# A chunked delta rule on one NeuronCore: the triangular inverse of levels 0 to 4 kept as 32-column blocks, and one set of square sums issued a chunk earlier

## The reference

```python
    sol = lax.linalg.triangular_solve(m, rhs, left_side=True, lower=True, unit_diagonal=True)
    u, w = sol[..., :dv], sol[..., dv:]
    qk = jnp.einsum('bhnid,bhnjd->bhnij', q, k) * decay
```

## Time and profile before

| | us |
|---|---|
| median of 3 runs | 1479.24 |
| the profiled execution, its own time | 1478.25 |
| its span, first to last instruction | 1476.4 |
| projection stage | up to about 344 |
| delta stage, four tiles | about 344 to 554 |
| its tail, mixing, experts, combining | the rest |
| mean granted TensorE clock | 0.988 |

### The profile page before, as it was taken

The page is one execution under the profiler, slowest core; times in us unless marked ns, Lnnn a source line. Parts: engine busy times, 40 slices in busy tenths (PEclk is TensorE's granted clock), DMA queues, the critical chain, the costliest instruction groups (busy, mean ns, idle before and its releaser), DMA issues. The chain is left out here.

```text
span 1476.4 us, 21155 instructions
## 1 busy us (share of the span) xinstructions
PE 1437.6 (97%) x8144; PEld 1143.3 (77%) x8144; DVE 973.3 (66%) x1765; ACT 625.8 (42%) x963; POOL 356.8 (24%) x236
## 2 busy tenths in 40 slices
PE   8999999998999999999899999999999999999986
PEld 6999999987998898788767667667667667767732
DVE  6648877515667676046978767767767767767628
ACT  3565333414244423011125555555555565565400
POOL 0000000004234340002463333333333333334200
PEclk9999999979999999999999999999999999999999
DMA  6222222210000002800739999999999999999767
GB/s 226 72 72 86 86 85 85 86 32 16 1 2 2 30 1 83 328 29 5 285 122 382 365 374 375 372 369 368 375 375 363 366 364 366 374 367 364 264 254 319
DMA packets 55932, 313.32 MB, mean 212 GB/s; under 512 B 15200, under 2 KB 16224, under 8 KB 36640
## 3 DMA queue, kind: packets, MB, share of 16 engines
q1 hardware_dynamic: 36080, 276.19, 49.5%
q0 software_dynamic: 19760, 35.89, 6.5%
HBM read 301.37 MB, written 42.12 MB: 233 GB/s over the span
## 5 line engine op out<-in xcount | busy, mean ns | idle before, releaser
L393 PE MATMUL bank<-x_hi,w_hi 128*128 128x274 f32 x768 | 230.4, 300 | 0.0
L2294 POOL DMA_INDIRECT expert_rows<-lru,slot_ids x64 | 155.9, 2435 | 297.8 <-DVE lru L2515 286.2
L395 PE MATMUL bank<-x_hi,w_lo 128*128 128x274 f32 x768 | 225.4, 294 | 0.0
L394 PE MATMUL bank<-x_lo,w_hi 128*128 128x274 f32 x768 | 224.5, 292 | 0.0
L2508 DVE TENSOR_TENSOR gate_up_lo<-wide,gate_up_hi 128x2048 fp32r<-128x2048 f32 x84 | 192.1, 2287 | 40.4 <-ACT gate_up_hi L2448 40.4
L2373 PE MATMUL bank<-gate_up_hi,rows_hi 128*128 128x512 f32 x512 | 206.3, 403 | 0.0
L2374 PE MATMUL bank<-gate_up_lo,rows_hi 128*128 128x512 f32 x512 | 200.3, 391 | 0.0
L2375 PE MATMUL bank<-gate_up_hi,rows_lo 128*128 128x512 f32 x512 | 200.0, 391 | 0.0
L2448 ACT ACTIVATE gate_up_hi<-wide 128x2048 fp32r<-128x2048 f32 x84 | 161.1, 1919 | 0.0
L394 PEld LDWEIGHTS bank<-x_lo,w_hi 128*128 128x128 f32 x768 | 147.7, 192 | 0.3
L393 PEld LDWEIGHTS bank<-x_hi,w_hi 128*128 128x128 f32 x768 | 146.9, 191 | 1.1 <-DVE w_lo L603 0.5
(11 more groups left out here) (358 smaller groups left out, 2583.0 us busy)
## 6 DMA issues: line engine op xcount, KB each, us to landing
wide<-in_w_exp SPq DMA_DIRECT2D x43, 2048.0 KB, 15.0
kept_wide<-in_w_exp SPq DMA_DIRECT2D x21, 2048.0 KB, 14.8
w_out_first<-in_w_in SPq DMA_DIRECT2D x48, 512.0 KB, 3.5
wide<-in_w_exp SPq DMA_DIRECT2D x22, 1024.0 KB, 13.1
w_out_first<-in_w_exp SPq DMA_DIRECT2D x21, 1024.0 KB, 13.4
kept_rows<-in_w_exp SPq DMA_DIRECT2D x21, 1024.0 KB, 13.3
expert_rows<-expert_rows SPq DMA_DIRECT2D x5, 1536.0 KB, 21.5
wide<-in_w_out SPq DMA_DIRECT2D x5, 1024.0 KB, 10.0
```

The source lines that it names most:

```text
L393: nc.tensor.matmul(out, wh[:, k, :], x_hi[:, k, at], start=(k == 0), stop=False)
L394: nc.tensor.matmul(out, wh[:, k, :], x_lo[:, k, at], start=False, stop=False)
L395: last = nc.tensor.matmul(out, wl[:, k, :], x_hi[:, k, at], start=False, stop=(k == DC - 1))
L2294: return pool.indirect_dma_start(out=dram["expert_rows"], out_offset=bass.IndirectOffsetOnAxis(ap=index, axis=0), in_=source, in_offset=No ...
```

## The change

In the projection stage the sums of tile 0 move from chunk 43 to chunk 42, and VectorE's read of them from its turn 44 to its turn 43.

In the delta stage, levels 0 to 4 no longer keep 128 by 128 inverses. After level 4 the inverse is block diagonal with blocks of 32, so each head's inverse is kept as 128 rows by 32 columns (`x_p`, and `x_t_p` for the transposed one). GpSimd masks `lower_t` to its 32 by 32 blocks (`mask_blocks`, in place of `begin_inverse`). TensorE then multiplies the 128 by 128 weights with 32 moving columns; VectorE's first half reads the product with a broadcast that spreads the 32 columns over four blocks; its second half subtracts 32 columns, and a 32 by 32 block transpose on VectorE (`turn_blocks`) gives `x_p`. TensorE's turn and ScalarE's copy are left at level 5 alone. Before level 5, GpSimd spreads both forms to 128 columns (`spread_inverse`, eight operations of 128x256). The transpose of level 0's second half becomes a matmul with a 32-column identity. The sample's first inverse (L1380) moves from VectorE to GpSimd. Smaller: one bias tile is four times narrower and read with a broadcast, the rows of log decays of the next tile wait for the last block product, and the constants grow by 160 columns.

```diff
-                project(pe, 40 + j, j, between={3: sum_prompt, 5: sum_sample}.get(j))
+                project(pe, 40 + j, j, between={2: sum_prompt, 5: sum_sample}.get(j))
...
-                elif n == 44:
+                elif n == 43:
                     rf.read(dve, 0)
...
+        lower_few_rows = carve(few_work, 0, H, BLOCK)
+        block_lower, rg_few = rg, o_sq
+        x_p = carve(mem.kept_wide, 4 * H * P, H, BLOCK)
+        x_t_p = [carve(work, 5 * H * P, H, BLOCK), *[lower_few_rows] * (TILES - 1)]
...
             def join_product(t, level):
...
+                        if level > SMALL:
+                            last = nc.tensor.matmul(inverse_bank(t, q, w)[:, h, :], lower_t[0:w, n, 0:w], x_inv[0:w, n, 0:w],
+                                                    start=True, stop=True)
+                        elif level:
+                            last = nc.tensor.matmul(blocks_out(t, q, 0)[:, h, :], block_lower[:, n, :], x_p[:, n, :],
+                                                    start=True, stop=True)
...
             def join_applied(t, level):
...
-                            last = nc.tensor.transpose(out, left, C("ident")[0:w, 0:w])
+                            last = nc.tensor.matmul(blocks_out(t, q, 1)[:, h, :], joined[:, n, :],
+                                                    x_t_p[t][:, n, :] if level else eye_p, start=True, stop=True)
...
-                    if 0 < level < LEVELS - 1:
-                        turn_inverse(t, level)
+                    if level == SMALL + 1:
+                        turn_inverse(t)
...
+            def mask_blocks(t):
+
+                for g, hs in groups:
+                    pool.wait_ge(s_u, 2 * turn(t) + g + 1)
+                    pool.tensor_tensor(block_lower[:, hs, :], lower_t[:, hs, :],
+                                       mem.delta_consts("blocks").unsqueeze(1).to_broadcast([P, 4, P]), ALU.mult)\
+                        .then_inc(s_bl, 1)
+
+            def spread_inverse(t):
+
+                mask = mem.delta_consts("blocks").unsqueeze(1).to_broadcast([P, 2, P])
                 for q, hs in pairs:
+                    pool.wait_ge(s_x, inverse_steps(t, SMALL, q))
+                    for small, out in ((x_p, x_inv), (x_t_p[t], x_inv_t[t % 2])):
+                        pool.tensor_tensor(by_block(out[:, hs, :]), spread(small[:, hs, :]), by_block(mask), ALU.mult)\
+                            .then_inc(s_un, 1)
...
                     scale_masks(t, 2, 3)
                     square_o(t - 1)
                     scale_masks(t, 4, 5)
+                    spread_inverse(t)
                     scale_o(t - 1)
...
             def join(t, level):
...
+                    if 0 < level <= SMALL:
+                        nc.vector.tensor_tensor(by_block(joined[:, hs, :]), spread(blocks_out(t, q, 0)), by_block(mask[:, hs, :]),
+                                                ALU.mult).then_inc(s_p, 1)
...
+                    for q, hs in pairs:
+                        dve.wait_ge(s_px, inverse_steps(t, level, q))
+                        nc.vector.tensor_tensor(x_t_p[t][:, hs, :], x_t_p[t][:, hs, :] if level else eye, blocks_out(t, q, 1),
+                                                ALU.subtract).then_inc(s_xtp, 1)
+                        if q:
+                            turn_blocks(t, level, q - 1)
+                    turn_blocks(t, level, 3)
                 after_joining(t, level)
+
+            def turn_blocks(t, level, q):
+
+                at = slice(2 * BLOCK * q, 2 * BLOCK * q + 2 * BLOCK)
+                dve.wait_ge(s_xtp, 4 * (SMALL + 1) * t + 4 * level + q + 1)
+                nc.vector.transpose(x_p.rearrange("p h c -> p (h c)")[:, at],
+                                    x_t_p[t].rearrange("p h c -> p (h c)")[:, at]).then_inc(s_x, 1)
```

More of the change, by code:

```diff
@@ L66 @@
 SUM_COLUMNS = 112
+SMALL, BLOCK = 4, 32
 CONSTS = {}
@@ L75 @@
 N_CONSTS = _at
-DELTA_CONSTS = {"masks": (0, LEVELS * P), "future": (LEVELS * P, P)}
-N_DELTA_CONSTS = (LEVELS + 1) * P
+DELTA_CONSTS = {"masks": (0, LEVELS * P), "future": (LEVELS * P, P), "blocks": (LEVELS * P + P, P),
+                "eye_blocks": (LEVELS * P + 2 * P, BLOCK)}
+N_DELTA_CONSTS = (LEVELS + 2) * P + BLOCK
 PARAMS = {}
@@ L836, in inverse_steps, with turned_steps, spread_steps, blocks_out @@
             return 4 * LEVELS * t + 4 * level + q + 1
-        def turned_steps(t, level, q):
-            return 4 * (LEVELS - 2) * t + 4 * (level - 1) + q + 1
+        def turned_steps(t, q):
+            return 4 * t + q + 1
+        def spread_steps(t, q, which):
+            return 8 * t + 2 * q + which + 1
+        def blocks_out(t, q, part):
+            return in_bank((row_banks(t) if q < 2 else key_banks(t)) + q % 2, P, BLOCK)[:, 2 * part:2 * part + 2, :]
+        def by_block(x):
+            return x.rearrange("p h (b c) -> p h b c", c=BLOCK)
+        def spread(x):
+            return x.unsqueeze(2).to_broadcast([P, 2, P // BLOCK, BLOCK])
         def mask_steps(t, level):
@@ L943, in join_product @@
                     for h in range(2):
-                        out, left = inverse_bank(t, q, w)[:, h, :], lower_t[0:w, 2 * q + h, 0:w]
-                        if level:
-                            last = nc.tensor.matmul(out, left, x_inv[0:w, 2 * q + h, 0:w], start=True, stop=True)
-                        else:
-                            last = nc.tensor.transpose(out, left, C("ident")[0:w, 0:w])
+                        n = 2 * q + h
+                        if level > SMALL:
[4 more added lines that the diff above has]
+                                                    start=True, stop=True)
+                        else:
+                            last = nc.tensor.transpose(inverse_bank(t, q, w)[:, h, :], lower_t[0:w, n, 0:w],
+                                                       C("ident")[0:w, 0:w])
                     last.then_inc(s_pa, 1)
@@ L955, in join_applied, with turn_inverse @@
                     pe.wait_ge(s_p, inverse_steps(t, level, q))
+                    if level == SMALL + 1:
+                        pe.wait_ge(s_un, spread_steps(t, q, 1))
                     for h in range(2):
-                        out, left = inverse_bank(t, q, w)[:, h, :], joined[0:w, 2 * q + h, 0:w]
-                        if level:
-                            last = nc.tensor.matmul(out, left, xt[0:w, 2 * q + h, 0:w], start=True, stop=True)
-                        else:
-                            last = nc.tensor.transpose(out, left, C("ident")[0:w, 0:w])
+                        n = 2 * q + h
+                        if level > SMALL:
+                            last = nc.tensor.matmul(inverse_bank(t, q, w)[:, h, :], joined[0:w, n, 0:w], xt[0:w, n, 0:w],
+                                                    start=True, stop=True)
+                        else:
+                            last = nc.tensor.matmul(blocks_out(t, q, 1)[:, h, :], joined[:, n, :],
+                                                    x_t_p[t][:, n, :] if level else eye_p, start=True, stop=True)
                     last.then_inc(s_px, 1)
-            def turn_inverse(t, level):
+            def turn_inverse(t):
                 w = tiles[t][2]
@@ L968, in turn_inverse @@
                 for q, _ in pairs:
-                    pe.wait_ge(s_x, inverse_steps(t, level, q))
+                    pe.wait_ge(s_x, inverse_steps(t, SMALL + 1, q))
                     for h in range(2):
@@ L1232, in _ @@
                 for level in range(1, LEVELS - 1):
-                    copy_inverse(t, level)
+                    if level == SMALL + 1:
+                        copy_inverse(t)
                     if t and level == 3:
@@ L1284, in log_decays @@
                 w = tiles[t][2]
-                if turn(t):
-                    pool.wait_ge(s_grow, 2 * turn(t))
-                pool.tensor_tensor(rg[0:w, :, 0:w], C("tri")[0:w, 0:w].unsqueeze(1).to_broadcast([w, H, w]),
+                if 0 < t < TILES:
+                    pool.wait_ge(s_pa, inverse_steps(t - 1, SMALL, 3))
+                pool.tensor_tensor((rg if t < TILES else rg_few)[0:w, :, 0:w], C("tri")[0:w, 0:w].unsqueeze(1).to_broadcast([w, H, w]),
                                    g_[0:w, t, :].unsqueeze(2).to_broadcast([w, H, w]), ALU.mult).then_inc(s_rg, 1)
@@ L1322, in _ @@
                         scale_masks(t, level)
+                        if level == 2:
+                            pool.wait_ge(s_p_few, 1)
+                            pool.tensor_tensor(x_inv_few[0:DEC], eye_few, joined_few[0:DEC], ALU.subtract)\
+                                .then_inc(s_xb_few, 1)
                         if level < levels_few:
                             scale_masks_few(level)
+                    spread_inverse(t)
                 scale_masks(t, 6)
@@ L1375, in few_step @@
                     dve.wait_ge(s_pa_few, level + 1)
+                    if level == 1:
+                        dve.wait_ge(s_xb_few, 1)
```

(28 more changed lines are left out.)

42 lines of the change are left out of this document (20 added, 22 removed).

## The result

The changed kernel takes 1498.91 us (median of 4 runs, 1497.51 to 1505.39), the kernel before beside it 1479.74 (4 runs). The ratio is 1.0138, with a 95% interval of 1.0108 to 1.0168: slower, by 19 to 20 us. The forecast had the sign, and the time is just inside the wider range (1461 to 1499) and above the forecast's own (1477 to 1495); but it put the loss at 7 us. The profiled execution is the longest of the four, 1505.39 us of its own time, so its parts add up to 6.5 us more than the median.

The account below looks back on a forecast made before the run. The prediction took TensorE to bound the stages touched. Full-clock terms of -13.8 us and a clock loss of +21.9 made +8.1, giving 1486 us; its own range was 1477 to 1495, the wider one 1461 to 1499.

Parts of the forecast that it names:

- all at full clock: Whole change with the clock at 1.00 throughout: sums -12.1, tile 0 -8.3, three later tiles +6.6, together -13.8 us.
- clock in tiles 1 to 3: Delta stage, later tiles: thin matmuls let the clock fall to 0.50, +6.3, +6.3 and +9.3, together +21.9 us.
- clock in tile 0: Delta stage, tile 0: the sample's matmuls fill in, so no clock loss was counted.
- rival 2: Delta stage: the clock falls in tile 0 as well, +13 us, giving 1499; chance 0.13.
- The square sums: Projection stage: VectorE's earlier read removes TensorE's hole in chunk 45 and chunk 46's low clock, -12.1 us.
- The matmuls of levels 1 to 4: Delta stage: weight loads set the pace, so a level's 32 instructions keep 3.6 us and only the turn goes.
- rival 4: Delta stage: thin matmuls hide their loads, VectorE sets every level at 3.0 instead of 3.6 us; 1462, chance 0.04.
- VectorE: Delta stage levels: first half keeps four operations; second has four subtractions and four block transposes, taken at 0.15 to 0.2 us.
- rival 3: Delta stage: block transposes cost 0.42 us, up to 0.8 a level in 16 levels, giving 1478; chance 0.05.
- Levels 4 and 5: Delta stage, tiles 1 and 2: GpSimd's eight spreads, with `o_factor` waiting behind them, cost +4.5 us a tile.
- Tile 0: Delta stage, tile 0 at full clock: L1380 leaves VectorE, turns go, the sample's chain starts earlier, -8.3 us.
- Rivals 1 and 5: Clock stays at 1.00: 1465, up to 1470, chance 0.35; VectorE's read of tile 0's sums still late: 1498, chance 0.03.

Follow-up runs that it names:

- four copies: Changed kernel with each matmul of levels 0 (second half) to 4 moving its 32 columns four times, so 128 columns; 1463.99 us, ratio 0.9886.
- four copies in tile 0: Changed kernel with the 32 moving columns given four times in tile 0 only, tiles 1 to 3 as in the changed kernel; 1483.62 us, ratio 1.0035.

## Why the prediction was right and wrong

| term | forecast, us | measured, us (by the ratios) |
|---|---|---|
| all at full clock | -13.8 | -16.9 (four copies, which still fall in level 5) |
| clock in tiles 1 to 3 | +21.9 | +22.0 |
| clock in tile 0 | 0 | +15.2 |
| sum | +8.1 | +20.3 |

The failed step is the last of the clock: "In tile 0 the sample's matmuls fill in; I take none there." They don't: the fall there cost 15.2 us (16.1 between the two traces), which the sum had at nothing. The clock fell there at the same point of the levels as in tile 1, and with four copies the same sample matmuls stand in a tile at 1.00. So it was the forecast together with rival 2, which I had priced at +13 and given 0.13. Its counterargument, that 32x32 matmuls keep the array moving, came from no row: the earlier trace rows show how long they take at 1.00, not what they do to the clock. Without such a row tile 0 should have been treated as the others.

That the term for tiles 1 to 3 came out to 0.1 us is in part luck. The mechanism was right, a fall in each. But the forecast's 6.3, 6.3 and 9.3 are 6.7, 4.5 and 7.1 by the traces (four copies in tile 0 less four copies), 18.3 in all, and 10.9 in place of 6.7 in the changed kernel's own trace. Nor is the kernel with four copies at full clock: it has 3 to 7 us at 0.50 in level 5 of these tiles, a part of which the forecast had counted under the clock.

*The square sums* gave 12 us by the run that has them alone, as forecast (-12.1); in the trace chunk 45 took 11.3 us, not 10.1.

*The matmuls of levels 1 to 4*: right at full clock, 16 in 1.95 us. The Trainium skill's floor of some 25 ns for small isolated matmuls (TensorE: Matmul & The Clock Gate, Back-to-back issue gap) is not what sets these: the trace has 0.112 us, with a load for each, and rival 4 falls. At 0.50 I took 0.19, between bounds; it is 0.213 (424.88 - 421.47, for 16), the upper one. (The prediction's 3.46 / 16 is 0.216, since 3.46 us hold the run-out of the last one.)

*VectorE*: a block transpose shows 0.24 us for one and 0.36 for two, 0.12 apart, a little under the 0.15 to 0.2; rival 3 falls. This is VectorE's timeline of the changed kernel, tile 0:

```profile
348.39 0.24 DVE L1491 STREAM_TRANSPOSE kept_wide<-delta_work 128x64 f32<-128x64 f32 x1
...
349.29 0.36 DVE L1491 STREAM_TRANSPOSE kept_wide<-delta_work 128x64 f32<-128x64 f32 x2
```

The levels came out nearly as worked out. This is TensorE's timeline of tile 1 with four copies, at the first product of levels 1 to 4 and 6:

```profile
401.15 1.95 PE L984 MATMUL bank<-kept_wide,delta_work 128*128 128x128 f32 x16
...
405.06 2.05 PE L984 MATMUL bank<-kept_wide,delta_work 128*128 128x128 f32 x16 [0.18 <-DVE kept_wide L1501]
...
412.33 1.96 PE L984 MATMUL bank<-kept_wide,delta_work 128*128 128x128 f32 x16
...
417.70 1.95 PE L984 MATMUL bank<-kept_wide,delta_work 128*128 128x128 f32 x16
...
431.42 1.96 PE L981 MATMUL bank<-delta_work 128*128 128x128 f32 x16
```

Level 1 takes 3.91 us (forecast 4.2), level 2 7.27 (7.2), level 3 5.37 (5.4), levels 4 and 5 13.72 (14.7).

*Levels 4 and 5*: the size was near, the reason half wrong. I let `o_factor` stand still until GpSimd's queue ran dry, as L1380 did. It did not: four of its operations lasted about as long as one spread each and went on with the next. The Trainium skill (SBUF — State Buffer, SBUF: two separate sides) has GpSimd and a VectorE operation with two SBUF inputs lock each other out for an instruction at a time; the three multiplications' 0.64 to 0.74 us agree (the factor's TENSOR_SCALAR, with one input, took 0.65 as well). My reading of L1380 was the harsher one; why L1380 let more than one GpSimd operation pass is not shown. The price was the spreads, plus a clock of 0.50 in or behind the wait for them.

*Tile 0* at full clock: -8.5 for the -8.3; L1380's move alone gave 4.3 for the 3.9 forecast.

Rivals 1 and 5 fall too: the clock did not stay at 1.00, and the read was no longer late.

## What to carry to other kernels

Here the weight load already set a matmul's pace, so that cutting its moving side from 128 columns to 32 saved nothing (16 in 1.95 us either way) and cost the clock, which every load behind it then paid (3.62 us); giving the columns back as copies cost no time. So look first at what sets the pace. Read the granted clock beside the busy share: TensorE was busy 100% at half clock. When one tile's clock has been forecast to fall, a neighbour with the same loads and columns needs a row of its own before it is taken out.

## What the runs showed that was not expected

With 128x128 loads 0.112 us apart, 32 moving columns were granted 0.50 in a part of all four tiles, 64 columns in tile 0 only, 128 columns in none (levels 0 to 4), while the waits and the sample's small matmuls were the same. It was not so at every level: levels 3 and 4 held 1.00 with 32 columns in tile 2, behind the sums, and in tile 1 they did in one profile and not in another. A load with 32 columns behind it doubles at 0.50 (3.62 us for 16, against 1.95 at 1.00). Some operations of 128x8 on VectorE take 0.65 us beside GpSimd's 0.72 us spreads, and 0.17 alone. The Trainium skill (TensorE: Matmul & The Clock Gate, Part 1) ties the clock to how busy the engine has been; the profile's busy share does not show it here, with 37.60 of 37.60 us at 0.50 and 24.00 of 24.00 at 1.00. Why 64 columns hold in tile 1 and not in tile 0, and why 32 hold in some levels, was not tried.
